# Six slots instead of eight in the ring of gathered expert rows

## The reference, cut to what matters

```python
u = expert_u[idx]                                   # 16 rows of 1024 per head and token
act = gelu(einsum('thkd,td->thk', u, h))            # one number per chosen expert
vv = expert_v[idx]
out = einsum('thk,thkd->td', gate * act, vv)        # weighted sum of 128 rows per token
```

## Time and profile before

| | us |
|---|---|
| three runs | 2720.12, 2723.48, 2711.39 |
| median | 2720.12 |
| profiled execution, its own time | 2712.26 |
| its span, first to last instruction | 2710.5 |
| PE busy | 2144.5 (79%) |
| DVE busy | 1550.5 (57%) |
| ACT busy | 1105.7 (41%) |
| POOL busy | 711.9 (26%) |

### The profile page before, as it was taken

The page is one execution under the profiler, slowest core; times in us unless marked ns, Lnnn a source line. Parts: engine busy times, 40 slices in busy tenths (PEclk is TensorE's granted clock), DMA queues, the critical chain, the costliest instruction groups (busy, mean ns, idle before and its releaser), DMA issues. The chain is left out here.

```text
span 2710.5 us, 31985 instructions
## 1 busy us (share of the span) xinstructions
PE 2144.5 (79%) x12228; PEld 1470.2 (54%) x12228; DVE 1550.5 (57%) x3382; ACT 1105.7 (41%) x2123; POOL 711.9 (26%) x621
## 2 busy tenths in 40 slices
PE   5889888787767756676657666778889799999998
PEld 2445478666546555555555555555558345444443
DVE  3476377635678755766566676547776664333204
ACT  1113221114576657666676666755553101111000
POOL 2000000002344324564555555433433500000000
PEclk8989879898889987666676677898899899999999
DMA  3301350325899998999999999999994312212120
GB/s 122 107 24 63 122 190 11 127 78 226 346 410 413 417 392 358 421 421 421 421 421 421 420 418 418 402 346 408 416 402 170 140 62 78 78 67 88 62 78 31
DMA packets 137978, 678.72 MB, mean 250 GB/s; under 512 B 9696, under 2 KB 12384, under 8 KB 71904
## 3 DMA queue, kind: packets, MB, share of 16 engines
q0 software_dynamic: 73728, 536.90, 48.3%
q1 hardware_dynamic: 64096, 139.76, 14.2%
HBM read 674.53 MB, written 2.10 MB: 250 GB/s over the span
## 5 line engine op out<-in xcount | busy, mean ns | idle before, releaser
L998 PE MATMUL PD<-C,AR 128*128 128x128 f32 x4096 | 732.5, 340 | 408.7 <-ACT AR L1382 407.8
L2304 POOL DMA_INDIRECT AR<-in_uv,C x512 | 637.4, 1245 | 1353.1 <-PE PD L998 708.0
L998 PEld LDWEIGHTS PD<-C,AR 128*128 128x128 f32 x4096 | 608.9, 176 | 576.9 <-ACT AR L1382 529.6
L2152 DVE CUSTOM_DVE_ANT_0 AR<-AR,HN 128x1024 f32<-128x1024 f32 x512 | 625.7, 1224 | 437.2 <-DMA AR<-in_uv,C 425.1
L1382 ACT ACTIVATE AR<-AR,SC 128x1024 f32<-128x1024 f32 x512 | 588.1, 1149 | 16.7
L607 PE MATMUL PA<-AR,WR 128*128 128x512 f32 (+1 forms) x656 | 283.5, 600 | 3.2 <-ACT AR L1229 3.2
L607 PEld LDWEIGHTS PA<-AR,WR 128*128 128x128 f32 (+1 forms) x656 | 125.2, 192 | 160.9 <-issue 159.7
L1378 ACT ACTIVATE SC<-SC 128x1 f32<-128x1 f32 x512 | 101.7, 199 | 225.4 <-DVE SC L2152 224.8
L972 PE MATMUL PA<-HT,WR 128*128 128x384 f32 x448 | 179.0, 527 | 0.0
L1380 ACT ACTIVATE SC<-SC,C 128x1 f32<-128x1 f32 x512 | 150.9, 295 | 16.6
L607 PE MATMUL PA<-HT,WR 128*128 128x128 f32 (+1 forms) x672 | 152.3, 387 | 2.3 <-DVE HT L2160 2.3
(11 more groups left out here) (426 smaller groups left out, 2430.6 us busy)
## 6 DMA issues: line engine op xcount, KB each, us to landing
WR<-in_w_in SPq DMA_DIRECT2D x18, 2048.0 KB, 13.9
WR<-in_w_ada SPq DMA_DIRECT2D x12, 2048.0 KB, 11.7
WR<-in_w_up SPq DMA_DIRECT2D x11, 2048.0 KB, 7.8
WR<-in_w_down SPq DMA_DIRECT2D x5, 2048.0 KB, 7.9
WR<-in_w_pq SPq DMA_DIRECT2D x4, 2048.0 KB, 23.9
AR<-in_uv,C POOLq DMA_INDIRECT x512, 14.4
AR<-in_w_pq SPq DMA_DIRECT2D x3, 2048.0 KB, 13.9
WR<-in_w_o SPq DMA_DIRECT2D x2, 2048.0 KB, 9.0
```

The source lines that it names most:

```text
L998: ins = nc.tensor.matmul(acc[i // 4][:, P * (i % 4):P * (i % 4) + P], UV[:, j, D + P * i:D + P * i + P], ident, start=(k == 0 and i % 4 == ...
L2152: ttr(UV[:, j, 0:D], UV[:, j, 0:D], HN[:, t, :], 1.0, 0.0, ALU.mult, ALU.add, DOT[:, j:j + 1]).then_inc(s["dots"], 1)
L2304: nc.gpsimd.indirect_dma_start(UV[:, ring_slot(turn), :], None, uv, bass.IndirectOffsetOnAxis(ap=IDX[:, t % 2, i:i + 1], axis=0),).then_in ...
```

## The change

The ring has six slots from the first turn on. The eighth slot, the numbering that changes from seven to eight at turn 28, and the one wait that belonged to it are gone.

```diff
-RING = 8
-SEVEN = 28
+RING = 6
 
 def ring_slot(turn):
-    return turn % 7 if turn < SEVEN else (turn - SEVEN) % RING
+    return turn % RING
 
 def ring_before(turn):
-    if turn == SEVEN + 7:
-        return None
-    before = turn - (7 if turn < SEVEN + 7 else RING)
-    return before if before >= 0 else None
+    return turn - RING if turn >= RING else None
 
 def ring_uses(turn):
-    before = ring_before(turn)
-    return 1 if before is None else 1 + ring_uses(before)
+    return 1 + turn // RING
...
                     if turn < 6:
                         pool.wait_ge(s["a_full"], FIRST_A["pq"] + 4 * (turn // 2) + 4)
-                    if turn == SEVEN + 7:
-                        pool.wait_ge(s["a_full"], FIRST_A["s"] + 4)
                     if ring_before(turn) is not None:
                         pool.wait_ge(s["uv_used"], ring_before(turn) + 1)
```

## The result

The changed kernel takes 2734.4 us in the median of 20 runs (2717.73 to 2741.58), the kernel before 2719.97 in 20 runs (2701.64 to 2727.09). The ratio is 1.0053, with a 95% interval of 1.0037 to 1.0070: 14.4 us slower, between 10 and 19. Forecast were 10.1 us, 2730.2, and a range of 2716 to 2748.

What follows compares the result with a forecast made beforehand. DMA transfers were taken to bound blocks 1 and 2, engines the holds and block 3. Blocks 1 and 2 at 0, two passages at 5.0 each and block 3 at 0.1 gave 2720.12 + 10.1 = 2730.2 us, range 2716 to 2748.

Steps and rivals of the forecast that it cites:

- blocks 1 and 2 at nothing: Middle of the ring, about 1063 to 1711 us: six slots cost 0, the shorter DMA queue hiding the change.
- spare of 4.5 us: Blocks 1 and 2: six slots leave 9.8 us from issue to landing, where a gather needs 5.3.
- The latency does not shrink (first rival): Blocks 1 and 2: 14.8 us latency is no queue, so 215 us more, time about 2935; chance 0.03.
- The price of a hold, two services once: Each passage from an engine-paced, empty DMA queue back to DMA-bound costs two gathers, 5.0 us; block 0 and change to 1.
- Block 3 at 0.1: Block 3: one tight turn makes PE 0.1 us late, with no passage back to a DMA-bound stretch.
- second rival: Block 3 loses as well: six weight chunks each make PE 1.5 us late, 9 us, time 2739; chance 0.24.
- All other turns have room: Block 3: apart from the one tightest turn found, later landings make no turn of PE late.
- The sum: Whole ring: 0 + 5.0 + 5.0 + 0.1 = 10.1 us slower, 2730.2 us, 0.37% more.
- Faster (last rival): Weight chunks wait up to 5 us less behind fewer queued gathers; at four chunks -10, time 2710; chance 0.02.
- partly absorbed: End of block 0, start of block 1: engines' backlog makes one passage free, sum 0 to 5, about 2723; chance 0.17.

Runs made afterwards that it cites:

- `depth`: Gathers alone, computation left out, 48 per depth of 1, 2, 3, 4, 6, 8 under way: 2.91 us a gather at depth 2, 2.61 at 3, 2.49 from 4 on.
- `hold6`: Changed kernel (six slots) plus 24 extra ACT copies in turn 200 of block 1; lag against the kernel before goes from 6.4 to 28.6 us.
- `six_late`: Kernel before with eight slots up to turn 147 and six from turn 148 on; lag -4.5 us at turn 150, -4.9 at 383, -3.3 at 511.
- `hold8`: Kernel before (eight slots) plus 24 extra ACT copies in turn 200 of block 1; lag goes from -3.0 to 15.5 us at turn 383.

## Why the prediction was right or wrong, point by point

**What bounds the kernel, and blocks 1 and 2 at nothing.** Right in the result: 238 issues against 239, a lag steady to 1 us from turn 150 to 383 in both profiles. The reason was wrong in one term. I gave a gather 5.3 us and six slots a spare of 4.5 us. The 5.3 us is the latency of a gather alone, and at that latency the stream does not run at full rate. At full rate it had 9.7 us (run `depth`), and at 7.3 us, with three under way, the rate was 5% down. So the need lies between these two, and the spare is between 0.1 and 2.5 us. Five slots, which by my term had 2.0 us to spare, lose a quarter of a microsecond in each turn. That six still fit was luck as far as this term goes: the same working would have called five free.

**The latency does not shrink (first rival).** It fell by 5.1 us, from 14.8 to 9.7. Refuted. The rule of the Trainium skill, *Perfetto Trace Analysis*, section "Optimization Strategy", says that the same gap repeated on the engine that should be saturated can mean too few buffers. At six slots the trace shows none in the middle, share 1.01. At four the engines are idle part of the time, share 0.92. At five the share is still 0.98 while the rate is down by 9%, so here the loss is seen in GB/s before it is seen as gaps.

**The price of a hold, two services once.** Supported in block 0 (5.3 us, four runs against four, counted from turns 38 to 49) and at the change from block 0 to 1 (5.4 us, four against four), by half of either with seven slots (2.5 each), by the hold put in (3.7 to 4.4), and by the holds taken out (1.5 us in the whole ring). The last two rest on one pair of profiles each.

**Block 3 at 0.1, second rival.** No cost beyond the scatter of 2 us, so the rival's 9 us did not come, and PE's idle time before its transposes, which was to decide, is 93.9 us in both windows. One reading was too wide. "All other turns have room" holds from turn 412 on. In turns 384 to 411 the same working comes out up to 4.9 us short. There the transfers still set the pace, and these turns carry the lag that was there already, so the sum does not change.

**The sum.** 10.1 us for the ring; the two profiles of the changed kernel have 10.6 and 9.9, and the two steps are 5.3 and 5.4. The other profiles lie up to 5 us under the one that I used as reference: with `hold6` up to its hold as a third for six slots, and `six_late` and `hold8` with the reference for eight, the difference of the means is 11.4 us at turns 150 and 180. The runs give 14.4, interval 10 to 19, and 10.1 lies at the lower end of that. Whether the few microseconds between are this or more executions with the slow attention stage, the runs don't settle. My sum had nothing for the time before the ring, where the profile has 11.8 us. Faster (last rival) and partly absorbed did not happen.

## What to carry to other kernels

Count the depth of a ring by the rate that its transfers keep with so many under way, measured by itself, and not by the latency of one of them alone: here one lands in 5.3 us, but four must be under way for the full rate. Slots beyond that paid only where an engine held the ring long enough to empty the queue, about one transfer each per hold. Shortening the holds was worth three to four times as much as the two slots (41 us against 14.4 by the times, 41.7 against 10.6 by the lags), and left 1.5 us for them to save in the ring.

## What the runs showed of the hardware that was not expected

- Indirect gathers of 128 rows of 8 KB: 182, 360, 402 and 422 GB/s with 1, 2, 3 and 4 under way, and no more with 6 or 8.
- The DMA share reads 0.98 at 360 GB/s as well as at 379 and 1.01 at 422: a share near 1 can hide a loss of 10 to 15% in rate.
- With five slots 23 GB/s and with four 32 GB/s are missing even against what the plain stream moved with as many gathers under way.
- Between 250 and 300 us, in the attention stage, the granted TensorE clock was 0.96 to 0.98 in some executions and 0.73 to 0.80 in others of code that is the same up to there, worth 7 to 12 us.
